# Two stacked models on one core: row inputs reordered, two mixers normed early, gate units between branch units, a split down-projection

## What is computed

```python
# first block, per layer: three attentions of 8 heads (forget gate, low rank, sliding window)
proj = rmsnorm(x, g) @ w_in
y_a, y_b, y_c = three_attentions(proj)            # causal, softmax
x = x + sum_n(sigmoid(gate_n) * (y_n * silu(z_n)) @ w_branch[n]) @ w_out
# second block, per layer
u = rmsnorm(x, g) @ w_in                          # 7964 columns, 4096 of them gates
y_ret = head_rmsnorm(retention(rq, rk, rv)) * silu(rg)
y_ssd = rmsnorm(ssd(silu(conv(xbc)), softplus(dt)) * silu(z))
y_gla = head_rmsnorm(gla(gq, gk, gv, log_sigmoid(ga @ w_alpha) / 16)) * silu(gr)
y_ml  = head_rmsnorm(mlstm(silu(conv(mqk)), mv, mi, log_sigmoid(mf))) * sigmoid(mo)
x = x + sum_n(sigmoid(gate_n) * y_n @ w_branch[n]) @ w_out
x = x + (silu(h @ w1) * (h @ w3)) @ w2            # layer 0; layer 1: experts
```

## Time and profile before

| | us |
|---|---|
| median of 3 runs (lowest, highest) | 2457.25 (2456.4, 2460.36) |
| profiled execution | 2457.24 |
| its span | 2455.4 |
| PE / DVE / ACT busy | 2289.9 / 1754.0 / 1299.6 |
| mean granted clock of TensorE | 0.974 |

### The profile page before, as it was taken

One profiled execution on the slowest core, in us unless ns is written; L12 is line 12 of the kernel. 1 busy time (PEld: TensorE's weight loads), 2 busy tenths in 40 slices (PEclk: granted clock), 3 DMA queues, 4 the chain that ended last, 5 costly groups with the idle time before them and its releaser, 6 DMA issues.

```text
span 2455.4 us, 38141 instructions
## 1 busy us (share of the span) xinstructions
PE 2289.9 (93%) x14926; PEld 1949.3 (79%) x14926; DVE 1754.0 (71%) x2743; ACT 1299.6 (53%) x1888; POOL 18.3 (1%) x37
## 2 busy tenths in 40 slices
PE   8999999999899698799998798789999999999998
PEld 7988789988788687699998687677777777777776
DVE  6556676566685557764456557759989889898896
ACT  5555546455453433342243434347767767777674
POOL 0000000000000000000000000000000000000000
PEclk9999999999999899999999899989999999999998
DMA  6432335443464333255444333249999999999993
GB/s 197 146 123 86 104 126 160 127 133 112 124 174 129 113 121 104 94 200 171 162 148 130 113 104 121 95 173 385 345 345 358 353 347 354 348 359 344 346 357 134
DMA packets 255496, 488.82 MB, mean 199 GB/s; under 512 B 35112, under 2 KB 208072, under 8 KB 221400
## 3 DMA queue, kind: packets, MB, share of 16 engines
q1 hardware_dynamic: 249792, 483.87, 57.0%
q0 software_dynamic: 656, 1.71, 0.2%
q10 hardware_dynamic: 4872, 0.81, 0.2%
HBM read 485.30 MB, written 1.05 MB: 198 GB/s over the span
## 4 chain that ended last, share of the span: by engine, by line
PE 68%; DVE 12%; ACT 3%; issue 2%; DMA 0%; DVEq 0%; ACTq 0%; SPq 0%
PE bank L1108 23%; PE bank L742 20%; PE bank L766 10%; PE bank L581 5%; DVE memr L2069 4%; PE bank L550 3%; ACT memr L1580 1%; DVE mem_high L2606 1%; DVE mem_high L2564 1%; PE bank L482 1%; PE bank L622 1%; DVE mem_high L2610 1%; PE bank L780 1%; PE bank L750 1%; PE bank L1062 1%
## 5 line engine op out<-in xcount | busy, mean ns | idle before, releaser
L1108 PE MATMUL bank<-memr 128*128 128x256 f32 (+6 forms) x7440 | 963.3, 289 | 82.1 <-DVE memr L2069 46.9
L1108 PEld LDWEIGHTS bank<-memr 128*128 128x128 f32 (+3 forms) x7440 | 914.7, 188 | 122.3 <-DVE memr L2069 50.2
L970 DVE TENSOR_TENSOR memr_tail<-mem_tail,memr_ring 128x2048 fp32r<-128x2048 f32 x198 | 448.3, 2286 | 32.9 <-ACT memr_ring L838 31.3
L742 PE MATMUL bank<-memr_ring,memr 128*104 128x512 f32 x1492 | 463.8, 396 | 1.4 <-DVE memr L977 1.4
L2069 DVE TENSOR_TENSOR memr<-mem_low,memr 128x1024 fp32r<-128x1024 f32 (+3 forms) x328 | 389.0, 1204 | 77.5 <-ACT memr L1580 76.6
L838 ACT CAST memr_ring<-mem_tail 128x2048 fp32r<-128x2048 f32 x198 | 375.2, 1914 | 77.5 <-PE bank L742 46.7
L1580 ACT CAST memr<-mem_low 128x1024 fp32r<-128x1024 f32 (+3 forms) x328 | 333.4, 1032 | 142.4 <-PE bank L1108 128.1
L742 PEld LDWEIGHTS bank<-memr_ring,memr 128*104 128x104 f32 x1492 | 251.5, 169 | 93.5 <-issue 1.5
L766 PE MATMUL bank<-memr_ring,memr 128*104 128x512 f32 x752 | 243.6, 402 | 1.0 <-DVE memr L1026 1.0
L742 PE MATMUL bank<-memr_tail,memr 128*104 128x512 f32 x536 | 211.6, 395 | 0.0
L766 PEld LDWEIGHTS bank<-memr_ring,memr 128*104 128x104 f32 x752 | 125.4, 168 | 43.1 <-issue 1.2
(11 more groups left out here) (298 smaller groups left out, 2329.0 us busy)
## 6 DMA issues: line engine op xcount, KB each, us to landing
mem_tail<-in_moe SPq DMA_DIRECT2D x198, 1024.0 KB, 4.9
mem_low<-in_w_in SPq DMA_DIRECT2D x112, 1024.0 KB, 5.2
mem_high<-in_moe SPq DMA_DIRECT2D x33, 1024.0 KB, 4.8
mem_low<-in_moe SPq DMA_DIRECT2D x33, 1024.0 KB, 4.9
mem_high<-in_ffn_w SPq DMA_DIRECT2D x30, 1024.0 KB, 8.9
mem_low<-in_w_branch SPq DMA_DIRECT2D x20, 1024.0 KB, 5.0
mem_low<-in_w_out SPq DMA_DIRECT2D x16, 1024.0 KB, 5.2
mem_low<-in_w_in SPq DMA_DIRECT2D x6, 512.0 KB, 3.7
```

Of the source, the lines that this page charges most:

```text
L742: ins = pe.matmul(ACC[g % 2][0:CAP, :], h_[e % 2][:, kk, :], w_[:, 512 * k:512 * k + 512], start=(kk == 0 and i == 0), stop=(kk == KT - 1 ...
L970: TTn(raw_r[n % RAW], raw[n % RAW], hi_f[n % HI], ALU.subtract).then_inc(family("m_split"), 1)
L1108: ins = pe.matmul(out(bank), lhsT, rhs, start=((k, i) == order[0]), stop=((k, i) == order[-1]))
```

## The change

1. **Front attention.** Keys are cut at 0-127, 128-255, 256-271 instead of 0-15, 16-143, 144-271. The product with V is 128 keys by 272 queries, 128 by 128, and two narrow ones of 16 keys by 32 queries. DVE copies 64 instead of 272 columns of 16 rows, and its bank is used in two halves. Transposes keep their number.
2. **Row inputs.** `gz 5` with `ga`, then `gz 7`, `mi`, `mf` come right behind `gz 3`; `al` behind `xbc 0`; `sdt` ends `xbc`; then `mv`, `gz 6`, `mqk`, `gz 4`, `gv`. DVE runs `conv_silu` two units behind `conv_sum`, and the row chain between `sdt` and `mqk`, with `low_with` calls in it. ACT runs the logarithms behind `sdt`. Most `low_after` of this part become `low_with`. One gate unit stands before the transposes and none behind.
3. **Norms.** The norms of `ret` and `ssd` get sums before the levels, roots behind them on ACT, and multiplications in level 1; the others behind the fourth branch unit. The results go to places of their own (`y2_places`).
4. **Levels.** `level_arg(n + 2)` is issued before `level_scaled(n + 1)`. The last pair uses bank XB.
5. **Gates.** Eight gate units stand between the units of branches 0 and 1. Branch weights come in chunks of 512 columns.
6. **Dense MLP.** `w2` and the hidden tile are split too: three fp32r matmuls for one f32, with `down_high`, `act_high` on ACT and `low_down` and a subtraction on DVE per tile.

```diff
...
 AHEAD = NHIGH * 2
 TT = [(0, META), (META, P), (META + P, P)]
+KEYS = [(0, P), (P, P), (2 * P, META)]
...
-        GATES_BEFORE = (3, 2)
...
+        NORM_SETS = (range(0, 3), range(3, 7))
+        NORMED = ((0, 1), (2, 3))
+        GATED = (1, 3)
...
+        def pair_bank(pair):
+            return XB if pair == 7 else OB
...
+        def down_parts(F):
+            c, f = next((c, F - f0) for c, (f0, nf) in enumerate(STEPS) if f0 <= F < f0 + nf)
+            return c, *(v[c % 3][:, 4096 + f * D:4096 + (f + 1) * D] for v in (mring, mring_r))
...
                 f0, nf = STEPS[c]
-                w = mring[c % 3][:, 4096:4096 + nf * D].rearrange("p (k c) -> p k c", k=nf)
-                pe.wait_ge(*at(f"mlp_w2_{c % 3}", c))
-                for f in range(nf):
-                    pe.wait_ge(*at("hidden", f0 + f))
+                for F in range(f0, f0 + nf):
+                    _, _, low = down_parts(F)
+                    high, a_h, a_l = w2_high[1][:, F % 4, :], act3_h[1][:, F % 3, :], act3_l[1][:, F % 3, :]
+                    pe.wait_ge(*at("w2_split", F))
+                    pe.wait_ge(*at("hidden", F))
                     for j in range(KT):
-                        ins = pe.matmul(YB[j // 2][:, (j % 2) * T:(j % 2 + 1) * T], w[:, f, j * P:(j + 1) * P],
-                                        actb[:, f0 + f, :], start=(f0 + f == 0 and j % 2 == 0),
-                                        stop=(f0 + f == NF - 1), skip_group_check=True)
-                ins.then_inc(*sig("mlp_down", c))
+                        for i, (w_, a_) in enumerate(((high, a_h), (low, a_h), (high, a_l))):
+                            ins = pe.matmul(YB[j // 2][:, (j % 2) * T:(j % 2 + 1) * T], w_[:, j * P:(j + 1) * P], a_,
+                                            start=(F == 0 and j % 2 == 0 and i == 0), stop=(F == NF - 1 and i == 2),
+                                            skip_group_check=True)
...
                 pe.wait_ge(*at("pt_act", g - 2))
             c = first_row(g // 24)
-            p = sm[g % 2]
-            for qt, (q0, nq) in enumerate(TT):
+            p, bank, side = sm[g % 2], TB[g % 2], XB[0:META, 2 * P * (g % 2):2 * P * (g % 2 + 1)]
+            for q0, nq in TT:
                 if not q0 and c:
                     continue
-                for kt in range(qt + 1):
-                    k0, nk = TT[kt]
-                    dst = (XB[0:nk, q0:q0 + nq], TB[g % 2][0:nk, q0 - META:q0 - META + nq],
-                           TB[g % 2][0:nk, 256:384])[kt]
-                    ins = pe.transpose(dst, p[0:nq, c + k0:c + k0 + nk], const("ident", nq)[:, 0:nq])
+                ins = pe.transpose(bank[0:min(P, q0 + nq), q0:q0 + nq], p[0:nq, c:c + min(P, q0 + nq)],
+                                   const("ident", nq)[:, 0:nq])
+                if q0 == META:
+                    ins = pe.transpose(side[:, 0:P], p[:, c + P:c + P + META], const("ident"))
+                if q0 > META:
+                    ins = pe.transpose(bank[:, TA:TA + P], p[:, c + P:c + 2 * P], const("ident"))
...
             lo = first_row(g // 24)
-            for t, nk, q0 in ((0, META, lo), (1, P, META), (2, P, META + P)):
+            for t, nk, q0, n in ((0, P, lo, TA - lo), (1, P, TA - P, P), (1, META, P - META, 32), (2, META, 2 * P - META, 32)):
                 for i in range(2):
                     v, v0 = ((vf, 64 * (hd + i)), (vm, 64 * (hd + i)), (vw, 64 * (hd // 4)))[kind]
-                    rhs = (ptx[(g + i) % 4][0:META, lo:], ptm[(g + i) % 4][:, 0:256], ptm[(g + i) % 4][:, 256:384])[t]
-                    ins = pe.matmul(OB[64 * i:64 * i + 64, q0:TA], v[0:nk, t, v0:v0 + 64], rhs,
+                    main, rest = ptm[(g + i) % 4], ptx[(g + i) % 4]
+                    rhs = main[:, q0 if t == 0 else TA:][:, 0:n] if nk == P else rest[0:META, 32 * (t - 1):32 * t]
+                    ins = pe.matmul(OB[64 * i:64 * i + 64, q0:q0 + n], v[0:nk, t, v0:v0 + 64], rhs,
                                     start=(t == 0), stop=(t == 2), skip_group_check=True)
...
                         rope2(("rk", l, j))
+                ch = split_chunk(win, l, 2692, 2836)
+                feat3(("gz", l, 5), ch, 0, P, T)
+                feat3(("ga", l), ch, P, 16, T)
+                ch = split_chunk(win, l, 3732, 3868)
+                feat3(("gz", l, 7), ch, 0, P, T)
+                feat3(("mi", l), ch, P, 4, T)
+                feat3(("mf", l), ch, P + 4, 4, T)
                 for j in range(6):
                     if j % 2 == 0:
                         ch = split_chunk(win, l, 1280 + j * P, 1280 + (j + 2) * P + (4 if j == 4 else 0))
                     feat3(("xbc", l, j), ch, j % 2 * P, P, T)
+                    if j == 0:
+                        pe.wait_ge(*evacuated("ga", l))
+                        c = pcol2[f"w_alpha{l}"][0]
+                        gemm(("al", l), [(par2[0:16, c:c + P], rowa[0:16, :])], lambda b: b[:, 0:T])
...
-                ch = split_chunk(win, l, 3732, 3868)
-                feat3(("gz", l, 7), ch, 0, P, T)
-                feat3(("mi", l), ch, P, 4, T)
-                feat3(("mf", l), ch, P + 4, 4, T)
...
-                ch = split_chunk(win, l, 2692, 2836)
-                feat3(("gz", l, 5), ch, 0, P, T)
-                feat3(("ga", l), ch, P, 16, T)
-                def alpha():
-                    pe.wait_ge(*evacuated("ga", l))
-                    c = pcol2[f"w_alpha{l}"][0]
-                    gemm(("al", l), [(par2[0:16, c:c + P], rowa[0:16, :])], lambda b: b[:, 0:T])
-                tok(("gv", l), split_chunk(win, l, 2308, 2564), 0, 256, alpha)
+                tok(("gv", l), split_chunk(win, l, 2308, 2564), 0, 256)
...
-                gate_units(GATES_BEFORE[0])
+                gate_units(1)
...
-                gate_units(GATES_BEFORE[1])
-                pe.wait_ge(*at("conv_ready", l, 9))
+                def norm_sums(part):
+                    pe.wait_ge(*at("o_squares", l, part))
+                    for i in NORM_SETS[part]:
+                        mat, feature_tiles = NORMS[i]
+                        gemm(("ssm", l, i), [(const(mat), squ[:, t, :]) for t in feature_tiles], lambda b: b[:, 0:T])
...
                 for i in range(12):
-                    g = 12 * l + i
+                    if i in (4, 8):
+                        pe.wait_ge(*at("conv_ready", l, 5 if i == 4 else 9))
...
+                norm_sums(0)
...
-                gate_units(2)
-                pe.wait_ge(*at("o_squares", l))
-                for k, (mat, feature_tiles) in enumerate(NORMS):
-                    gemm(("ssm", l, k), [(const(mat), squ[:, t, :]) for t in feature_tiles], lambda b: b[:, 0:T])
-                gate_units(3)
+                gate_units(1)
                 for n in range(4):
-                    ch = split_pieces(a["w_branch_2"][l, n], 2, D, (0, 512, D))
...
-                        feat3(("br2", l, n, j), ch, j * P, P, T, slots=(2 * n, 2 * n + 1),
+                        if n == 0 and j == 4:
+                            norm_sums(1)
+                        if j % 4 == 0:
+                            ch = split_pieces(a["w_branch_2"][l, n][:, j * P:(j + 4) * P], 2, 512, (0, 512))
+                        feat3(("br2", l, n, j), ch, j % 4 * P, P, T, slots=(0, 1), src=y2_places[n][1:],
                               key=None if j else ("branch2", l, n))
+                        if n < 2 and j % 4 in GATED:
+                            gate_units(1)
...
+                gate2(l, 5)
+                copy_unit(rowa[0:16, :], ("ga", l), slice(0, 16))
+                gate2(l, 7)
+                follow("mf", l)
+                def conv_tanh(j):
+                    act.wait_ge(*at("conv_sum", l, j))
+                    if j >= 2:
+                        act.wait_ge(*at("conv_ready", l, j - 2))
+                    st(A(asc[:, 2 + j % 2, 0:T], conv[:, j, :], ACT.Tanh, scale=0.5), sig("conv_tanh", l, j))
...
-                for t in range(2):
-                    copy_unit(vtok[:, 3, t, :], ("mv", l, 2, t), slice(0, P))
-                gate2(l, 6)
...
+                    if j:
+                        conv_tanh(j - 1)
+                conv_tanh(5)
+                follow("sdt", l)
+                act.wait_ge(*evacuated("sdt", l))
...
+                for t in range(2):
+                    copy_unit(vtok[:, 3, t, :], ("mv", l, 2, t), slice(0, P))
+                gate2(l, 6)
+                for j in range(4):
+                    copy_unit(mqk[:, j, 3:T + 3], ("mqk", l, j), slice(0, P))
+                    if j:
+                        conv_tanh(5 + j)
+                gate2(l, 4)
+                conv_tanh(9)
+                for t in range(2):
+                    copy_unit(vtok[:, 2, t, :], ("gv", l, t), slice(0, P))
...
+                def norm_roots(part):
+                    act.wait_ge(*at("o2_done", l, part))
...
+                    st(A(squ[:, four, :], o2[:, four, :], ACT.Square), sig("o_squares", l, part))
...
+                norm_roots(0)
```

(86 more changed lines are left out.)

238 lines of the change are left out of this document (114 added, 124 removed).

## The result

Before 2456.82 us (4 runs), after 2423.41 us (2421.41 to 2426.86, 4 runs): ratio 0.9862, 95% interval 0.9845 to 0.988. The change is faster by 33.4 us (1.4%); the forecast was 69.

What follows compares the result with a forecast made beforehand. PE, busy 93% of the span, was taken as the bound. From 2457.2, two layers at -26 (row inputs) and 0 (levels, norms, branches), -10.6 (MLP) and -6.7 (attention) gave 2388 us (2371 to 2405; wide range 2350 to 2426).

Steps and rivals of the forecast that it cites:

- rival A: Conv stage and levels 1 to 3: waits only move, clock falls in new gaps, 12 saved a layer; 2416 us, 28%.
- Row inputs, -26: Mixer stage before the first score: early gates and a reordered row chain cut PE's waits, 26 us less per layer.
- The 3 us kept for the clock: Row inputs: 3 us per layer allowed for lower PE clock after the longer new waits.
- Levels: Norm sums, nine gates, nine levels and waits take 44.4 us, with 2.4, 1.3 and 3.2 before levels 1 to 3.
- Branches 0 and 1, 41: With eight gate units and second norm sums, these branches run at PE's pace and take 41 us.
- DVE's 30 us hide in it: Branches 0 and 1: DVE's 30 us of mixes, sums, tiles, norms and lows hide in 41 us.
- The prediction's own sign for this stage: Branches 0 and 1 with gate units take some 40 us with PE over 90% busy.
- Its sign of being wrong: The forecast is wrong if DVE reaches 90% in either window: row inputs, or levels, norms and branches.
- Branches 2 and 3, 20.3: The last two branches stay at DVE's pace and take 20.3 us, as before.
- MLP, -10.6: Dense MLP: split down-projection saves 14.1 us, the start comes 3.5 later, so 10.6 us less.
- Front attention, -6.7: First block: fewer streamed columns save 0.28 us for each of 24 pairs, 6.7 us; transposes keep number and widths.
- C: Ten convolution units: ACT and DVE wait for each other without overlap, 7.7 us per unit; slower, 2484 us, 5%.

Runs made afterwards that it cites:

- the first experiment: The changed kernel with the second norm block cut in two, each half on VectorE while PE works on a gate unit: 2406.93 us, ratio 0.979.

## Why the prediction was off

The measured 2423 lies 18 us above the forecast's own upper bound (2405) and just inside the wide range (2350 to 2426), which reached that far for rival A's sake. The mechanism ahead of the scores was right, and so were the experts, the scores and the levels. The stage behind the levels was wrong by 38 us in the two layers, which is the whole difference of 35 and a little more; the other errors nearly cancel.

- **Row inputs, -26: right, and short by 5.** The waits were forecast as 1.6, 0.9, 1.1, 3.9 and 2.5 and are 1.7, 0.7, 1.1, 3.3 and 0.6 in all. The 0.6 for the bank of `al` didn't come, nor did the 1.0 in the rope part: the 0.67 and 0.37 that stand there now stood there before (0.66 and 0.37). The 3 us kept for the clock weren't needed: 0.98 in this window, 0.90 before.
- **Levels: the sum right, by luck.** 44.3 us to the end of the levels, forecast 44.4; 2.95 before the first branch unit, forecast 2.8. But the waits before levels 1 to 3 are 2.3, none and 1.5, where 2.4, 1.3 and 3.2 were forecast, and instead one gate unit took 5.48 at the lower clock. In layer 1, at full clock but for one unit, the waits are 2.3, none and 2.9. The 1.4 at the first norm sums, for ScalarE's table load and logarithm, came in neither layer.
- **Branches 0 and 1, 41: wrong, 54.5.** The step that failed is "DVE's 30 us hide in it". I compared sums, 41 of PE against 30 of VectorE, and never asked what stands in front of the multiplication that frees the bank, though I had walked the queues unit by unit in the row inputs. I had "2 of small waits"; it was 10.5, and the other 5 are the lower clock behind them (0.84): PE's busy time is 43.8, and 38.8 at full clock in the first experiment. With the order mended the same work takes 43.6. (The terms add up to 40.2, not 41.) The prediction's own sign for this stage, PE over 90% busy, came out as 80% (43.8 of 54.5). Its sign of being wrong, VectorE at 90%, did not come: VectorE is busy for 71% and 68% of the two windows. A share of busy time can't see this error.
- **Branches 2 and 3, 20.3: short by 2.9.** I took them as unchanged. A chunk of 512 columns is one tile, and with a ring of two chunks VectorE is two tiles ahead instead of four: five subtractions fall into these 16 units instead of three. The narrow chunks also put a wait of 2.6 before the last unit, which the wide ones don't have. Part of the error is in the 20.3 itself, a window from 1022.9 to 1043.2: the 192 matmuls of the 32 branch units lie between 1000.74 and 1041.13, so the window starts inside branch 2 and ends inside the output projection. The spacing of the rows gives some 20.9 for the 16 units. The output projection, which I had as unchanged, takes 25.0 from its first matmul where it took 23.5; in the seven profiles with wide chunks here it takes 23.5 to 23.9, in the seven with narrow ones 23.9 to 25.2.
- **MLP, -10.6: the saving was mis-sized.** 7.07 and 11.58 are lengths to the modelled end of the last matmul; from start to start 16 products in f32 take 6.72 and split 5.74, so 10.8 is saved, not 14.1. The up products between them gained another 1.8 (11.36 instead of 11.53, ten times). Against 3.5 of waits at the start, 1.5 came there (2.15 where 0.69 was), and 1.7 before a late down tile and 1.1 before the next layer, where I had none. Alone it is worth 5.4, half of the forecast.
- **Front attention, -6.7: near in number (-6.0 alone), and partly by luck.** A pair's products save 0.23 each instead of 0.28, 5.5 in all. The transposes, put at nothing, went from 0.58 to 0.63 per head, which costs 2.4. That leaves 3.1. In the part's own profile PE's busy time up to the first mixer is 4.7 less and its gaps are 0.9 shorter; the other 1.6 of busy time I can't assign.
- **Rivals.** The time came out near rival A's 2416, but not by its mechanism: it moved the waits inside the row inputs and lost the gain there. What happened was nearest to the lesson of C, engines in order that stand in front of each other, in a place where I had not looked for it.

The Trainium skill (Perfetto Trace Analysis, Matmuls) says that independent matmul groups should rotate through different PSUM banks, so that one group's evacuation overlaps the next one's matmuls. Here that is so for as long as the next group lasts: at 976.57 the evacuation came 8.5 us after its unit was done, the gate unit in the other bank covered 3.0 of them, and PE waited for 5.6. A third bank was not tried, so whether it would have hidden the rest isn't shown.

## What to carry over

When work is moved beside other work, compare orders, not sums: for every buffer that the bounding engine needs back, list what stands in the freeing engine's queue ahead of the instruction that frees it, with the waits of these instructions. With two buffers, as here, the cover is one unit of the bounding engine (3.0 us), however idle the other is over the whole stage (VectorE was busy for 29 of 54); a block of small instructions goes where the freeing has just been done, not in front of it. And an interleaving is to be measured against the plain block: here the block was faster by 12 to 14 us until the order inside the interleaving was right, and as fast (2396.9 against 2396.3) once both had been mended.

## What was not expected of the chip

- The clock fell behind the same wait of 1.8 us in some executions and not in others (20 matmuls in 4.29 or in 2.78), also between kernels with one and the same first block. Two profiled executions can differ by 3 us in one stage for that reason alone, so a part of 6 us needs its own timed runs.
- A logarithm followed by an exponential costs ScalarE two table loads of 1.28 us each, and the first use starts within 0.02 us of the load's end. The further 1.4 us per norm wait, 6 in all, that the prediction worked out as an alternative are in no trace. The wait of 2.02 before the second norm sums, in the experiment with the multiplication first, is such a load and the logarithm of the sums before. ScalarE at the second norms of the changed kernel:

```profile
957.60 1.28 ACT L1945 ACT_TABLE_LOAD   x1
...
962.01 1.28 ACT L1949 ACT_TABLE_LOAD   x1
963.30 1.06 ACT L1949 ACTIVATE mem_high<-mem_high 128x1024 f32<-128x1024 f32 x1
```

- A split product costs 0.120 per matmul of 256 columns from start to start (48 in 5.74), an f32 one 0.42 (16 in 6.72): three for one save 15%, not the 18% that lengths gave.
- Six transposes of unchanged widths, cut at 128 instead of 16 keys, take 0.63 instead of 0.58 us.
